# Attention steps in pairs in a hybrid decoder block on eight cores: two weighted sums, two sets of scores, three projection items

## The reference

```
u = rms_norm(x)
q, k, v, z, g_att, g_pool = split(u @ w_in)           # 24 heads of 64: 3 dilation groups x 8 heads
q, k = partial_rope(q), partial_rope(k)               # the first 16 of 64 dims of each head
for g, (w, d) in enumerate(((128, 1), (512, 4), (2048, 16))):
    # each query sees the keys at distances 0, d, 2d, ..., w
    s = q_g . k_g * 64**-0.5 ;  m = max(s) ;  p = exp(s - m) ;  l = sum(p) ;  o_g = p @ v_g / l
o = sum_g softmax_g(m + log l) * o_g                  # per head slot, over the 3 groups
merged = sigmoid(g_att) * (o @ w_att) + sigmoid(g_pool) * (pool(z) @ w_pool)
h = x + merged @ w_out
h = h + (silu(f @ w_gate) * (f @ w_up)) @ w_down      # f = rms_norm(h)
out = rms_norm(h)
```

## Time and profile before

| | |
|---|---|
| median of 3 runs | 1263.28 us (1260.54 to 1264.37) |
| the profiled execution | 1261.55 us, span of its slowest core 1260.0 us |
| spans of the 8 cores | 1243.1 to 1260.0 us |
| TensorE (PE) busy | 1179.1 us, 94% of the span, 8328 matmuls |
| VectorE (DVE), ScalarE (ACT) busy | 519.4 us (41%), 454.2 us (36%) |
| mean granted TensorE clock of the cores | 0.985 to 0.991 |
| chain that ended last | PE 83%, DMA 7%, DVE 5%, ACT 3% |

### The profile page before, as it was taken

One profiled execution on the slowest core, in us unless ns is written; L12 is line 12 of the kernel. 1 busy time (PEld: TensorE's weight loads), 2 busy tenths in 40 slices (PEclk: granted clock), 3 DMA queues, 4 the chain that ended last, 5 costly groups with the idle time before them and its releaser, 6 DMA issues.

```text
span 1260.0 us, 21152 instructions; the slowest of 8 cores (1243.1 to 1260.0 us)
## 1 busy us (share of the span) xinstructions
PE 1179.1 (94%) x8328; PEld 643.7 (51%) x8328; DVE 519.4 (41%) x778; ACT 454.2 (36%) x718; POOL 68.9 (5%) x134
## 2 busy tenths in 40 slices
PE   3897899999999998979997999999999999999997
PEld 1454666576676664534443444444444444444466
DVE  3454555555544449765432445211113211222343
ACT  2554655845754655561221122111122032111211
POOL 0001000000001010101020000000000000000000
PEclk9999999999999999999998999999999999999999
DMA  7854723233224320304594021334702713445722
GB/s 182 242 174 102 172 67 72 51 74 79 64 49 89 73 46 14 76 1 78 132 184 92 16 52 34 68 67 89 131 7 53 140 34 67 78 82 100 175 101 84
DMA packets 31680, 109.94 MB, mean 87 GB/s; under 512 B 4704, under 2 KB 9056, under 8 KB 25696
## 3 DMA queue, kind: packets, MB, share of 16 engines
q0 software_dynamic: 15264, 69.76, 28.9%
q1 hardware_dynamic: 16320, 38.84, 10.6%
HBM read 148.31 MB, written 16.06 MB: 130 GB/s over the span
## 4 chain that ended last, share of the span: by engine, by line
PE 83%; DMA 7%; DVE 5%; ACT 3%; issue 2%; POOL 0%; DVEq 0%; SPq 0%; ACTq 0%; POOLq 0%
PE ps_p L197 46%; PE ps_s L197 19%; PE ps_o L197 15%; PE ps_o L200 3%; DMA pb<-wpb 3%; DMA wp<-w_in 1%; DVE uto L210 1%; DMA xs<-x 1%; DVE uth L210 1%; DMA qk<-rout 1%; ACT pt L204 1%; ACT rs L204 1%; DMA rout<-rp 0%; DVE acc L207 0%; ACT uth L204 0%
## 5 line engine op out<-in xcount | busy, mean ns | idle before, releaser
L197 PE MATMUL ps_p<-uto,wp 128*128 128x512 bf16 x768 | 182.4, 387 | 11.1 <-DVE uto L210 5.4
L197 PE MATMUL ps_s<-ftv,wguv 128*128 128x512 bf16 x640 | 144.7, 379 | 0.0
L197 PE MATMUL ps_o<-ftv,wguv 128*128 128x512 bf16 x640 | 144.7, 379 | 0.0
L207 DVE TENSOR_TENSOR pt<-pt,msk_s 128x1024 bf16<-128x1024 bf16 x96 | 66.0, 690 | 146.7 <-ACT pt L204 146.7
L197 PEld LDWEIGHTS ps_p<-uto,wp 128*128 128x128 bf16 x768 | 72.7, 99 | 102.0 <-issue 23.0
L197 PE MATMUL ps_p<-actt,wdv 128*128 128x512 bf16 (+1 forms) x616 | 115.5, 349 | 2.0 <-DVE actt L207 2.0
L204 ACT ACTIVATE pt<-ps_s 128x1024 bf16<-128x1024 f32 x96 | 98.3, 1024 | 22.5 <-PE ps_s L197 18.8
L197 PEld LDWEIGHTS ps_o<-ftv,wguv 128*128 128x128 bf16 x640 | 62.6, 98 | 75.5
L197 PEld LDWEIGHTS ps_s<-ftv,wguv 128*128 128x128 bf16 x640 | 62.6, 98 | 75.5
L204 ACT ACTIVATE qk<-ps_p 128x512 bf16<-128x512 f32 (+1 forms) x120 | 69.1, 584 | 88.0 <-PE ps_p L197 68.1
L197 PE MATMUL ps_p<-wp,uto 128*128 128x128 bf16 x1536 | 97.2, 223 | 0.0
(11 more groups left out here) (114 smaller groups left out, 1362.7 us busy)
## 6 DMA issues: line engine op xcount, KB each, us to landing
wguv<-wgu POOLq DMA_DIRECT2D x20, 1024.0 KB, 8.4
wp<-w_in POOLq DMA_DIRECT2D x12, 768.0 KB, 7.7
wdv<-wd POOLq DMA_DIRECT2D x6, 1408.0 KB, 17.3
ht<-x SPq DMA_DIRECT2D x32, 256.0 KB, 7.9
xs<-x SPq DMA_DIRECT2D x3, 2048.0 KB, 20.7
xs<-x POOLq DMA_DIRECT2D x3, 2048.0 KB, 11.1
xs<-x SPq DMA_DIRECT2D x4, 1024.0 KB, 11.7
oT<-ost SPq DMA_DIRECT2D x12, 256.0 KB, 2.8
```

What stands on the lines that cost most here:

```text
L197: return P.op("pe", lambda e: e.matmul(out, lhsT=lhsT, rhs=rhs, start=start, stop=stop), after)
L207: return P.op("dve", lambda e: e.tensor_tensor(out=out, in0=in0, in1=in1, op=op), after)
```

## The change

From the first step up to the end of unit 11's first items the steps are taken two at a time (`pair_mode`). A pair issues the weighted sums of both steps of the pair before, then two sets of scores, the first into `ps_s` and the second into the upper two banks of `ps_p`, and then asks for three items. While that holds, items have two banks instead of four, and `finish` is called once for each pair instead of once for each step. Afterwards banks and steps go on as before. The number and the shapes of the instructions stay as they were.

```diff
-    nbank = [0]
+    nbank, banks = [0], [4]
     def take_bank():
-        k = nbank[0] % 4
+        k = nbank[0] % banks[0]
...
-    s_free = [None]
+    s_free = [[None], [None]]
...
-    def scores(u, s):
+    def scores(u, s, k=0):
         g = u % 3
+        ps = (ps_s[:, :], ps_p[:, 1024:2048])[k]
...
-                    t = mm(ps_s[:, o:o + 128], qk[g][pr, 2048 + 128 * kb:2048 + 128 * kb + 128],
-                           qk[g][pr, 128 * b:128 * b + 128], True, True, after=[t_rope[u], s_free[0]])
-        t = act(pts[i], ps_s[:, :], AF.Exp, after=[t, pt_free[i]], scale=0.125)
-        s_free[0] = t
+                    t = mm(ps[:, o:o + 128], qk[g][pr, 2048 + 128 * kb:2048 + 128 * kb + 128],
+                           qk[g][pr, 128 * b:128 * b + 128], True, True, after=[t_rope[u]] + s_free[k])
+        t = act(pts[i], ps, AF.Exp, after=[t, pt_free[i]], scale=0.125)
+        s_free[k] = [t]
...
+    def pair_mode(on):
+        banks[0] = 2 if on else 4
+        nbank[0] = 0
+        if on:
+            s_free[1] = bank_free[2:4]
+        else:
+            bank_free[2:4] = s_free[1] * 2
+
     def do_step():
-        if len(pend) > 1:
-            weighted(pend.pop(0))
-        u, s = steps.pop(0)
-        scores(u, s)
+        if banks[0] == 2:
+            while pend:
+                weighted(pend.pop(0))
+            for k in range(2):
+                scores(*steps.pop(0), k)
+            since[0], need[0] = 0, 3
+        else:
+            if len(pend) > 1:
+                weighted(pend.pop(0))
+            u, s = steps.pop(0)
+            scores(u, s)
+            since[0], need[0] = 0, 1 + s % 2 * spread[0]
         if norm_q:
             finish(*norm_q.pop(0))
-        since[0], need[0] = 0, 1 + s % 2 * spread[0]
...
+            if steps[0] == (0, 0):
+                pair_mode(True)
             do_step()
...
     finish_turns()
+    pair_mode(False)
```

More of the change, by code:

```diff
@@ L796, in _body @@
     mfree = [None, None]
-    pfree = [[s_free[0], s_free[0], o_free[0], o_free[1]], list(bank_free)]
+    pfree = [[s_free[0][0], s_free[0][0], o_free[0], o_free[1]], list(bank_free)]
     t_mg = {}
```

## The result

The changed kernel takes 1271.82 us (median, 1271.28 to 1272.21) against 1263.67 of the kernel before beside it: the two medians differ by 8.15 us, where 8.4 were forecast (1271.7). The ratio on record is 1.0077, with a 95% interval of 1.0056 to 1.0098: 9.7 us, between 7.1 and 12.4. In some executions of a kernel the cores of one half of the chip show a lower granted clock throughout and the time is several per cent longer; the ratios leave these out, the medians given with the experiments don't. The profiled execution has a span of 1269.9 us on core 6, and the cores lie between 1255.1 and 1269.9.

A forecast was written before the change was run, and what follows sets the result against it. TensorE bounds the long stage, busy 286.64 of 290 us. Removed 12.0 (8.6 + 3.4), added 20.4 (16.1 + 2.5 + 0.6 + 1.2): 8.4 us slower than the median 1263.28, so 1271.7, range 1260 to 1286.

The forecast's parts named there:

- The passages and the scores' waits: Attention on TensorE: fewer switches between scores and other matmuls save 8.6 us, scores no longer waiting for the exponential 3.4.
- The rival that charged 4 us for it: Pair's second set of scores pays a passage of its own: 4 us more, 1276; chance 0.05.
- The third item's wait: In 12 pairs with a normalisation, item three waits for ScalarE's copy of item one to free its bank: adds 16.1 us.
- (a): First pair: the input's last statistics get their bank late, TensorE idles and its clock falls: adds 2.5 us, 0.8 to 4.2.
- (b): End of the first unit: weighted sums follow the last scores with no item between, waiting 3.0 against 2.4: adds 0.6 us.
- (c): Five pairs hold a short item, so some matmuls come before their bank or input is ready: adds 1.2 us, 0 to 3.
- The clock rival: Nine repeated item waits bring TensorE's clock to 0.50 each time, costing 14 us more: 1286; chance 0.13.
- The two rivals that left out all or half of the waits: Item three's waits absent, 1255.6, chance 0.09; or half, 7.5 in place of 16.1, no change at 1263, chance 0.11.

The follow-up runs named there:

- e1: The changed kernel with the normalisation (`finish`) issued behind a pair's first item instead of ahead of it; 1256.08 us, ratio 0.9948 to the kernel before.
- e4: e1 with weighted sums and scores alternating inside a pair instead of two of each in a row; 1262.78 us, ratio 1.0004 to the kernel before.
- e2: The kernel before, steps still single, but items go round two banks instead of four while attention runs; 1267.38 us, ratio 1.0033.
- e7: The changed kernel with two normalisations at a pair instead of one, giving six longer waits in place of twelve; 1278.21 us, ratio 1.0137 to the kernel before.

## Why the prediction was right

The mechanism came out as forecast, and the terms lie near their places. That 1271.7 met 1271.8 to 0.1 us is luck all the same: by the table the mean core is 10.2 later at the end of attention, counted from the first step (10.0 + 0.2), where the sum had 8.4, and by the ratio on record it is 9.7. Of the 1.8 between 8.4 and 10.2 the waits make 1.7.

- **The passages and the scores' waits (8.6 and 3.4).** 36 of the 40 pairs lie behind unit 0: 7.7 + 3.4 = 11.1. The changed kernel loses 7.6 there (2.4 to 10.0) with waits of 17.8 and two of the short items' of 0.55, so the pairs give back 11.3; e1 gains 9.4 (2.5 to -6.9) with waits of 1.4 and the same 1.1, so 11.9. e4 gives the passages behind unit 0 as 7.0, against 6.8. The second set of scores pays no passage: it starts 0.24 after the first (233.48 to 233.72) and four times 0.056 are 0.22. The rival that charged 4 us for it is out. The Trainium skill (TensorEngine Tiling (Array Packing), Key Properties) says that a change of tiling mode, not of the tile, drains TensorE; the 0.24 between sets of one mode and the 0.55 and 0.33 of e4 across modes agree.
- **The third item's wait (16.1).** By the spacing of starts it is 17.8. Changed against e1, which keeps 1.4 of it, the three clusters differ by 5.7, 5.2 and 5.6 (4.6 + 1.1 and so on): 16.5. Behind two long items the wait is 1.71, as worked out. What the sum had too small is the waits behind small items: it gave 32 small matmuls 2.04, read at one place in unit 0, and on core 1 they take 1.82 in the first cluster (218.37 to 220.19, shown above). So item three asks for its bank 0.2 earlier for each such item ahead of it. The first waits of the clusters are 1.06, 1.01 and 1.01, where 0.83, 0.55 and 0.55 were forecast, and two of the others 1.64 in place of 1.40.
- **(a) The statistics (2.5, 0.8 to 4.2).** 4.0 measured, near the upper end. The idle time is 3.2 to 6.6 us on the 8 cores, not 4.4. On six of them the eight matmuls of the statistics take about 3.4, at 0.50 as feared; on core 3 they take 2.26, and on core 2, behind an idle time of 3.30, 1.72 at 1.00. 1.4 of the 4.0 is back by the end of unit 0, in e2 with its single steps as well: in the kernel before some matmuls there go at the pace of VectorE's `uth` (on core 5 those at 141.17, 141.83 and 142.49, each after a wait of 0.29 us), and the kernels that come to them later have one such wait or none. The net of 2.6, which holds (b) and the gain of unit 0's pairs too, is near the 2.5.
- **(b) The end of unit 0 (0.6).** The two waits are 2.53 and at most 0.2 against 2.55 and 0.46, so 0.1 to 0.3 over the 2.4 of before.
- **(c) The short items (1.2).** Two waits of 0.55 by the spacing of starts, 1.1.
- **The clock rival.** Not inside the clusters: 96 waits, none with a lower clock. The Trainium skill (TensorE: Matmul & The Clock Gate, A second HAM failure mode: psum-queue depth-cycling) tells of short idle times between groups that bring the clock down again and again; it did not come about at 1.55 us in every 8.45, and did at half of e7's 2.9 to 3.6.
- **The two rivals that left out all or half of the waits** needed ScalarE's chain to be shorter than its rows. Every spacing of it came out within 0.02 us.

## What to carry to other kernels

When banks are taken from a ring to serve something else, follow the queue of the engine that frees them, in program order, from the event that starts it to the copy that is asked for; the rows of before gave that chain to 0.02 us. Then ask which link in it has nobody waiting: here the normalisation, which one line moves behind the copy, and a loss of 8 us becomes a gain of about 7. Count the matmuls in a row against the matmuls that the program has, and time a wait by the spacing of starts: a missing record looked like a late start, and the idle time in brackets left out 0.16 us of every wait. A change that loses as a whole may hold a gain and a cost that come apart.

## What was not expected of the hardware

The granted clock let 96 waits of up to 1.6 us (by the profile's idle time) pass in the changed kernel, and came down with half of the 48 waits of 2.9 to 3.6 us in e7, with waits of equal length on either side of that: on core 0 the one that ended at 455.11 (3.50) has it, the one that ended at 343.17 (3.50) has not. The stretch tables of the two, with the clock third from the end:

```profile
454.00:460.80 6.80, 5.70 (x34) 3.29 (x36) 5.23 (x11) 2.36 (x5) 0.00 (x0) 0.50 0.05 8
343.20:350.00 6.80, 6.75 (x56) 3.75 (x58) 6.22 (x15) 4.25 (x6) 0.00 (x0) 1.00 0.35 69
```

What tells the two apart is not shown by these runs.
